# Two residual blocks with a mixture of experts on one core: the router with its weights stationary, the tokens' parts by quarters, the overflow count in eight parts, the gathers in other steps

## The reference

```python
def moe_swiglu(h, router, w1, w3, w2):        # h [256, 1024], 8 experts, top 2, d_ff 3584
    logits = (h @ router).astype(jnp.float32)
    top_v, top_i = lax.top_k(logits, TOP_K)
    gates = jax.nn.softmax(top_v, axis=-1).astype(h.dtype)
    ...
    def expert_block(args):
        xe, e = args
        return swiglu(xe, w1[e], w3[e], w2[e])    # (silu(x w1) * (x w3)) w2
    ...
    y = zeros.at[row_tok].add(yb * row_w[:, None])
```

## Time and profile before

| what | value |
|---|---|
| median of 3 runs | 2162.42 us (2159.96 to 2165.96) |
| profiled execution | 2167.47 us, its span 2166.1 us |
| granted TensorE clock, mean over the span | 0.976 |
| PE busy | 2086.6 us (96%) |
| DVE busy | 1711.0 us (79%) |
| ACT busy | 1260.6 us (58%) |
| chain that ended last | PE 84%, DVE 9%, ACT 4%, issue 3% |
| HBM traffic over the span | 267 GB/s |

### The profile page before, as it was taken

The page is one execution under the profiler, slowest core; times in us unless marked ns, Lnnn a source line. Parts: engine busy times, 40 slices in busy tenths (PEclk is TensorE's granted clock), DMA queues, the critical chain, the costliest instruction groups (busy, mean ns, idle before and its releaser), DMA issues.

```text
span 2166.1 us, 30863 instructions
## 1 busy us (share of the span) xinstructions
PE 2086.6 (96%) x12783; PEld 1859.6 (86%) x12783; DVE 1711.0 (79%) x1845; ACT 1260.6 (58%) x1270; POOL 39.8 (2%) x77
## 2 busy tenths in 40 slices
PE   5999999899999999999999999999999999999997
PEld 4887899899898999999998788887888878888886
DVE  6777696899767776777547888897898978898886
ACT  3457643545334454443446677776777767777775
POOL 3010000000000000000000000000000000000000
PEclk8999999899999999999999999999999999999999
DMA  9853576467763446888536999998999989999993
GB/s 307 274 164 111 171 240 205 148 213 251 235 204 136 155 151 210 296 280 276 186 125 243 324 349 365 359 360 317 354 364 357 359 314 353 360 366 366 359 372 148
DMA packets 332802, 580.73 MB, mean 268 GB/s; under 512 B 10357, under 2 KB 150155, under 8 KB 332656
## 3 DMA queue, kind: packets, MB, share of 16 engines
q1 hardware_dynamic: 329152, 572.57, 75.9%
q0 software_dynamic: 3008, 5.78, 1.2%
q10 hardware_dynamic: 496, 0.33, 0.1%
HBM read 577.56 MB, written 1.07 MB: 267 GB/s over the span
## 4 chain that ended last, share of the span: by engine, by line
PE 84%; DVE 9%; ACT 4%; issue 3%; DMA 0%; SPq 0%; DVEq 0%; ACTq 0%
PE bk L632 14%; PE bk L634 14%; PE bk L633 14%; PE bk L626 9%; PE bk L627 9%; PE bk L628 9%; DVE macc L1863 3%; DVE wlo L1836 2%; ACT whi L1256 2%; PE bk L703 1%; PE bk L1148 1%; PE bk L688 1%; PE bk L689 1%; PE bk L690 1%; DVE uc L2182 1%
## 5 line engine op out<-in xcount | busy, mean ns | idle before, releaser
L1836 DVE TENSOR_TENSOR wlo<-raw,whi 128x2048 fp32r<-128x2048 f32 x475 | 1081.0, 2277 | 281.2 <-ACT whi L1256 280.4
L1256 ACT CAST whi<-raw 128x2048 fp32r<-128x2048 f32 x475 | 902.6, 1901 | 405.4 <-PE bk L634 271.1
L626 PE MATMUL bk<-HH,whi 128*128 128x256 f32 x1480 | 430.4, 291 | 6.9 <-DVE HL L1909 6.2
L627 PE MATMUL bk<-HL,whi 128*128 128x256 f32 x1480 | 421.2, 285 | 0.0
L628 PE MATMUL bk<-HH,wlo 128*128 128x256 f32 x1480 | 420.8, 284 | 0.0
L632 PE MATMUL bk<-whi,xh 128*128 128x512 f32 x896 | 357.2, 399 | 4.9 <-DVE wlo L1836 4.9
L634 PE MATMUL bk<-wlo,xh 128*128 128x512 f32 x896 | 351.2, 392 | 0.0
L633 PE MATMUL bk<-whi,xl 128*128 128x512 f32 x896 | 350.7, 391 | 0.0
L626 PEld LDWEIGHTS bk<-HH,whi 128*128 128x128 f32 x1480 | 286.6, 194 | 11.4 <-issue 8.7
L627 PEld LDWEIGHTS bk<-HL,whi 128*128 128x128 f32 x1480 | 286.7, 194 | 1.6 <-issue 1.0
L628 PEld LDWEIGHTS bk<-HH,wlo 128*128 128x128 f32 x1480 | 286.4, 194 | 0.0
(11 more groups left out here) (366 smaller groups left out, 2606.4 us busy)
## 6 DMA issues: line engine op xcount, KB each, us to landing
raw<-in_moe_w SPq DMA_DIRECT2D x336, 1024.0 KB, 6.1
raw<-in_ada_w SPq DMA_DIRECT2D x48, 1024.0 KB, 5.3
raw<-in_ff_w SPq DMA_DIRECT2D x40, 1024.0 KB, 5.3
raw<-in_w_in SPq DMA_DIRECT2D x29, 1024.0 KB, 5.5
raw<-in_w_mod SPq DMA_DIRECT2D x24, 1024.0 KB, 5.6
raw<-in_w_up SPq DMA_DIRECT2D x22, 1024.0 KB, 5.1
raw<-in_attn_w_qkv SPq DMA_DIRECT2D x12, 1024.0 KB, 5.2
raw<-in_w_branch SPq DMA_DIRECT2D x8, 1024.0 KB, 5.3
```

The lines of the kernel that those rows point to most:

```text
L626: pe.matmul(o, sh, mh, start=start, stop=False, skip_group_check=True)
L627: pe.matmul(o, sh, ml, start=False, stop=False, skip_group_check=True)
L1256: act.copy(whi[k][:, :n], raw[q.slot[i]][:, :n]).then_inc(q.hi_done.mark(g), 1)
L1836: dve.tensor_tensor(wlo[k][:, :n], raw[q.slot[i]][:, :n], whi[k][:, :n].bitcast(F), ALU.subtract).then_inc(q.taken.mark(i), 1)
```

## The change

1. The logits: the router's chunk is stationary and all 256 tokens of H2 move, so the logits come out as 8 x 256. DVE copies them to SBUF (`LT`, in a part of `onat`), TensorE transposes them in two small transposes into a second bank ("lgt"), and DVE reads them there.
2. The tokens' transposes go by `quarters`: first the low four chunks of both halves, then the high four. The two small transposes stand behind the first quarter. DVE computes the first two quarters of TL ahead of the ranks, the other two behind PB. The first gather waits for two quarters at its chunk 0 and for the other two at its chunk 4, and has 4 spare matmuls ahead of it in place of 14.
3. The cast (ACT) and the split (DVE) of slab 138 + NP move to the end of the route, on ACT behind the exponential, on DVE behind the gates.
4. `dve_count` takes a part number and runs in steps 2 to 9, one part in each.
5. The gathers for the next pair are in steps i = 5, 6, 7 and 12, the gather's rest in step 13.

```diff
+        LT = onat[0:8, 0, 0:S]
...
+        quarters = ((0, 0), (1, 0), (0, 4), (1, 4))
+        gather_at = {5: 0, 6: 2, 7: 4, 12: 6}
...
@@ pe_route @@
-            for tb in range(2):
-                for k in range(8):
-                    pe.wait_ge(*(yield from act_step.of("h2", k)))
-                    t = pe.matmul(u.t[:, 8 * tb:8 * tb + 8], H2[:, k, tb * 128:tb * 128 + 128], rw[:, k, :], start=(k == 0), stop=(k == 7))
+            for k in range(8):
+                pe.wait_ge(*(yield from act_step.of("h2", k)))
+                t = pe.matmul(u.t[0:8, 0:S], rw[:, k, :], H2[:, k, :], start=(k == 0), stop=(k == 7))
             t.then_inc(u.fill(), 1)
-            for tb in range(2):
-                for c in range(0, 8, 4):
-...
+            for n, (tb, c) in enumerate(quarters):
+                u = take(X_G, "tok", tb, c)
+                for j in range(4):
+                    t = pe.transpose(u.t[:, j * 128:(j + 1) * 128], H2[:, c + j, tb * 128:tb * 128 + 128], ident)
+                t.then_inc(u.fill(), 1)
+                if n == 0:
+                    u = take(X_L, "lgt")
+                    pe.wait_ge(*(yield from N.of("lt")))
+                    for tb in range(2):
+                        t = pe.transpose(u.t[:, 8 * tb:8 * tb + 8], LT[0:8, tb * 128:tb * 128 + 128], ident[0:8, 0:8])
                     t.then_inc(u.fill(), 1)
...
@@ pe_gather @@
             if q is st and p == 0:
-                spare(us[0].t[:, 0:128], 14)
-                for n in range(4):
-                    pe.wait_ge(*(yield from N.of("tl", n)))
+                spare(us[0].t[:, 0:128], 4)
             pe.wait_ge(*(yield from dve_step.of("pb", q.name, p)))
             for c in chunks:
+                if q is st and p == 0 and c in (0, 4):
+                    for n in (c // 2, c // 2 + 1):
+                        pe.wait_ge(*(yield from N.of("tl", n)))
...
 @@ pe_experts (act_experts and dve_experts alike) @@
-                if p < 3 and 4 <= i < 8:
-                    yield from pe_gather(st, p + 1, M_T, (2 * i - 8, 2 * i - 7))
-                if p < 3 and i == 12:
+                if p < 3 and i in gather_at:
+                    yield from pe_gather(st, p + 1, M_T, (gather_at[i], gather_at[i] + 1))
+                if p < 3 and i == 13:
...
@@ act_route @@
-            yield from act_hi(st, 138 + NP)
-            for n in range(4):
-                tb, c = n // 2, n % 2 * 4
+            for n, (tb, c) in enumerate(quarters):
...
             act.activation(col(3), col(2), AF.Exp).then_inc(act_step.mark("gap"), 1)
+            yield from act_hi(st, 138 + NP)
...
@@ dve_route @@
-            yield from dve_lo(st, 138 + NP)
...
+            dve.tensor_copy(LT, u.t[0:8, 0:S]).then_inc(u.sem, 1)
+            N.note(("lt",), u.drained())
+            dve.wait_ge(*(yield from B.full("lgt")))
+            u = B.at["lgt",]
...
+            for n in range(2):
+                yield from tokens_low(n)
             dve.wait_ge(*(yield from B.full("rank")))
...
             yield from dve_pb(st, 0, lambda n, tb: RK[:, tb, n:n + 1])
-            for n in range(4):
-...
+            for n in range(2, 4):
+                yield from tokens_low(n)
...
             dve.tensor_tensor(gt, gt, tmp, ALU.add).then_inc(dve_step.mark("gates"), 1)
+            yield from dve_lo(st, 138 + NP)
...
 @@ dve_experts @@
-                if s_ == 2:
-                    yield from dve_count()
+                if 2 <= s_ < 10:
+                    yield from dve_count(s_ - 2)
```

More of the change, by code:

```diff
@@ L1079, in pe_route @@
             pe.wait_ge(*(yield from N.of("rw")))
-            for tb in range(2):
-                for k in range(8):
-                    pe.wait_ge(*(yield from act_step.of("h2", k)))
-                    t = pe.matmul(u.t[:, 8 * tb:8 * tb + 8], H2[:, k, tb * 128:tb * 128 + 128], rw[:, k, :], start=(k == 0), stop=(k == 7))
+            for k in range(8):
+                pe.wait_ge(*(yield from act_step.of("h2", k)))
+                t = pe.matmul(u.t[0:8, 0:S], rw[:, k, :], H2[:, k, :], start=(k == 0), stop=(k == 7))
             t.then_inc(u.fill(), 1)
-            for tb in range(2):
-                for c in range(0, 8, 4):
-                    u = take(X_G, "tok", tb, c)
-                    for j in range(4):
-                        t = pe.transpose(u.t[:, j * 128:(j + 1) * 128], H2[:, c + j, tb * 128:tb * 128 + 128], ident)
+            for n, (tb, c) in enumerate(quarters):
[8 more added lines that the diff above has]
+                        t = pe.transpose(u.t[:, 8 * tb:8 * tb + 8], LT[0:8, tb * 128:tb * 128 + 128], ident[0:8, 0:8])
                     t.then_inc(u.fill(), 1)
@@ L1771, in act_experts @@
                     yield from act_collect(st, s_ - 1, e - 1, (e - 1) // 2, (e - 1) % 2)
-                if p < 3 and 4 <= i < 8:
-                    yield from act_gather(st, p + 1, (2 * i - 8, 2 * i - 7), True)
-                if p < 3 and i == 12:
+                if p < 3 and i in gather_at:
+                    yield from act_gather(st, p + 1, (gather_at[i], gather_at[i] + 1), True)
+                if p < 3 and i == 13:
                     yield from act_ptt(st, p + 1)
@@ L2415, in dve_route, with tokens_low @@
             dve.tensor_tensor(col(2), col(1), col(0), ALU.subtract).then_inc(dve_step.mark("gap"), 1)
+            def tokens_low(n):
+                tb, c = quarters[n]
+                dve.wait_ge(*(yield from xhi_done.of("tok", n)))
+                u = B.at["tok", tb, c]
+                dve.tensor_tensor(TL[:, tb, c * 128:c * 128 + 512], u.t[:, :], TH[:, tb, c * 128:c * 128 + 512].bitcast(F),
+                                  ALU.subtract).then_inc(u.sem, 1)
+                N.note(("tl", n), u.drained())
+            for n in range(2):
+                yield from tokens_low(n)
             dve.wait_ge(*(yield from B.full("rank")))
@@ L2497, in dve_scatter, with dve_count @@
                     t.then_inc(dve_step.mark("x_moe"), 1)
-        def dve_count():
+        def dve_count(part):
             eix = misc[:, 256:264]
[L2502 to L2513, removed]
+            if part == 0:
+                dve.wait_ge(*(yield from B.full("count")))
+                u = B.at["count",]
+                dve.tensor_copy(CN[:, 0:8], u.t[:, 0:8]).then_inc(u.sem, 1)
+                dve.wait_ge(*u.drained())
+                dve.tensor_scalar(CN[:, 8:16], CN[:, 0:8], float(CAP), None, ALU.is_gt).then_inc(dve_step.mark("ov"), 1)
+                dve.memset(CN[:, 56:64], 1.0).then_inc(dve_step.mark("ov"), 1)
+                dve.wait_ge(*dve_step.now())
+                dve.tensor_tensor_scan(CN[:, 16:24], CN[:, 56:64], CN[:, 8:16], 0.0, ALU.mult, ALU.add).then_inc(dve_step.mark("ov"), 1)
+                dve.wait_ge(*dve_step.now())
+                dve.tensor_copy(CN[:, 48:49], CN[:, 23:24]).then_inc(dve_step.mark("ov"), 1)
+                dve.memset(OV[:, :, 3:4], -1.0).then_inc(dve_step.mark("ov"), 1)
+                return
+            if part == 7:
+                dve.wait_ge(*(yield from dve_step.of("ov")))
+                dve.tensor_copy(CI[:, :], CN[:, 48:52]).then_inc(dve_step.mark("ci"), 1)
+                return
+            j = (part - 1) // 2
+            sj, ej = CN[:, 24 + 8 * j:32 + 8 * j], CN[:, 49 + j:50 + j]
+            dve.wait_ge(*(yield from dve_step.of("ov")))
+            if part % 2:
                 dve.tensor_scalar(sj, CN[:, 16:24], float(j + 1), None, ALU.is_equal).then_inc(dve_step.mark("ov"), 1)
@@ L2522, in dve_count @@
                 dve.tensor_scalar(ej, ej, 7.0, None, ALU.min).then_inc(dve_step.mark("ov"), 1)
[L2523 to L2532, removed]
+                return
+            for tb in range(2):
+                dve.wait_ge(*dve_step.now())
+                dve.tensor_tensor_reduce(CN[:, 56:64], sj, RK[:, tb, :], 1.0, -float(CAP), ALU.mult, ALU.add,
+                                         OV[:, tb, j:j + 1]).then_inc(dve_step.mark("ov"), 1)
+                dve.wait_ge(*dve_step.now())
+                dve.tensor_tensor_reduce(CN[:, 56:64], sj, ro(tb, 7), 1.0, 0.0, ALU.mult, ALU.add,
+                                         OV[:, tb, 4 + j:5 + j]).then_inc(dve_step.mark("ov"), 1)
         def dve_experts():
```

## The result

The median went from 2163.89 us (four runs, 2159.96 to 2165.96) to 2139.95 (four runs, 2139.00 to 2141.42): ratio 0.9889, 95% interval 0.9872 to 0.9905. The forecast was 2141, range 2135 to 2150.

The account below looks back on a forecast made before the run. TensorE's matmuls set the experts' pace, so gains had to come from its waits. Gains of 6.7 + 11.8 + 4.6, less 0.5 for holds and 1.0 for the clock, gave 21.6 us: median 2162.4 to 2140.8, say 2141, range 2135 to 2150.

Parts of the forecast that it names:

- The count: Experts, step after the count, 23.69 us and 6.73 too much: spreading the count over steps 2 to 9 gains 6.7 us.
- 0.5 us allowed for new holds: Experts, steps 2 to 9: the inserted count parts hold TensorE up by 0.5 us in all; bounds 0 and 8.
- the slack read off at 1450.64: Experts, DVE: work inserted there put the next split 2.17 us later, yet its step took the undisturbed 17.46 us.
- The gathers: Experts, two two-step stretches with turns waiting for a bank: moving the gathers gains 5.55 + 6.29 = 11.8 us; bounds 7.4, 11.8.
- The route: Ahead of the experts, from logits to first expert: the shorter chain gains 4.6 us; bounds 6.8 and 1.6.
- 1.0 off for the clock: Experts' start: a low clock there costs 1.0 us; bounds 0 and 3.
- step (f): Route, gather: chunks 6 and 7 wait for banks emptied by DVE's XL copies, a hole of 2 us before chunk 6.
- a low stretch inside the gather: Route: hidden behind DVE, as six chunks would then take 5.7 us and end at 1142.6.
- Rival 1: Route: clock low from the rank to about 1148, experts start 3 us later, gain near 19, time 2144; chance 0.13.
- Rival 2: Experts: DMA can't hold 369 GB/s, most of the 18.5 us return as ACT's waits, time near 2158; chance 0.05.
- Rivals 3 and 4: Experts, steps 12 and 13: bank wait once per pair, 2159 us, chance 0.05; waits in both steps, 2176 us, chance 0.02.
- The sum: Whole kernel: 6.7 + 11.8 + 4.6 - 0.5 - 1.0 = 21.6 us gained.

Follow-up runs that it names:

- e5_count_halves: Kernel after, with the count's eight parts run four in step 2 and four in step 3; single execution 2145.16 us.
- e4_one_chunk: Kernel after, with the gathers' chunks 1, 2, 2, 2 and 1 in steps 4, 5, 6, 7 and 12; single execution 2139.45 us.
- e1_count: Kernel before, with only the count split into eight parts; median 2157.27 us, ratio to before 0.9973.
- e3_route: Kernel before, with only the new route (count and gathers as before); median 2155.01 us, ratio to before 0.9968.
- e11_after_again: Kernel after once more, unchanged, beside e9_spare_late; median 2141.84 us, ratio to before 0.9896.
- e2_gathers: Kernel before, with only the gathers moved to steps 5, 6, 7 and 12, their rest to 13; median 2152.29 us, ratio to before 0.9955.
- e6_old_logits: Kernel after, with the logits in their old form, without the copy and the two small transposes; single execution 2137.62 us.
- e8_spare: Kernel after, with three more spare matmuls ahead of the rank and seven in place of four ahead of the gather; single execution 2143.59 us.
- e9_spare_late: Kernel after, with the spare matmuls of e8_spare and DVE's third-slab split moved behind the XL copies; median 2140.45 us, ratio to before 0.9889.
- e7_slab_early: Kernel after, with the third slab's cast and split back in their old early place in the route; single execution 2145.98 us.

## Why the prediction was right

**The count** was to give 6.7 us: step 3 fell by 6.69. The 0.5 us allowed for new holds was not needed. DVE's heaviest piece (collection, part 5 and the turn's low part, in its program for step 7) runs from 1278.20 to 1280.98 in the profile after, which is behind the turn at 1274.80; the step from there to the next turn takes 17.47, against 17.46 before. So 2.8 us went unnoticed there, and the slack read off at 1450.64 in the earlier trace rows holds. e5_count_halves shows its end: 5.05 us of DVE work between two splits cost a wait of 2.5.

**The gathers** were to give 5.55 and 6.29. The two stretches of the earlier trace rows fell by 6.46 (41.87 to 35.41) and by 7.3, and steps 12 and 13 of the same pairs took on the 0.9 that was moved there: 5.5 and 6.3. That the bank was the cause is shown by e4_one_chunk. The size of the loss varies from execution to execution: what a pair of steps lost beyond its wait of 3.7 us was 5.55 - 3.7 = 1.9 and 6.29 - 3.7 = 2.6 us in the profile before, and by the steps' lengths in the same way (against 36.32) 1.9 and 0.2 in e1_count, 2.6 and 1.8 in e3_route. The bare waits, 7.4 us, are in all three; of the other 4.4, e1_count would have shown only 2.1. The varying part goes with the clock: from the end of the wait to the end of the pair it was granted at 1.00 on average where 0.2 us was lost, at 0.91 in the three cases with 1.8 or 1.9, and at 0.87 and 0.88 in the two with 2.6. So the prediction's assumption that every execution loses the full 11.8 does not hold; that it came out so near is in part luck.

**The route** was to give 4.6 with 1.0 off for the clock, 3.6; it gave 4.1. Up to the gather the sum holds to 0.1 us: lg copied at +4.50 (forecast 4.6), gather at +9.69 (9.8 to 9.9). Behind that two things came otherwise. In e11_after_again, with the clock at 1.00, the hole of step (f) is there with 1.6 us (2 forecast), but chunk 6 begins at +14.42 where the sum has 14.9, and the first expert comes at +16.72 where it has 17.2: several differences of about 0.1 us, all to the good. (The XL copies take 0.34 each when free to run, eight in 2.74, not 0.47; only the first of them stands in the sum, and chunk 6 began 0.47 after its start.) And in the profile after the low clock fell inside the gather and reached nearly to its end: chunk 6 began at 1138.97, with the XL copies already on their way, so the hole was not there, and the first expert came 0.8 us later than in e11_after_again. The prediction had called a low stretch inside the gather hidden behind DVE. By its own figures (six chunks at the low clock end at 1142.6, the bank is free at 1141.9) it would be hidden only in part. So the 1.0 us taken off for the clock had about the right size, 0.8, but it was lost in the gather and not, as reckoned, under the first experts.

**Rival 1** (the clock stays low from the rank into the first expert) came about in part: low through the gather, back at 1.00 before the first expert matmul. In after the clock was 1.00 in the stretch with the transposes (1128 to 1130) and fell only near 1133 (0.98 from 1132 to 1133, 0.50 from 1133 to 1134): behind the wait of 1.4 us, and ahead of the one of 0.6 us, which ended at 1133.68. By the rule of the Trainium skill ("TensorE: Matmul & The Clock Gate", Part 4) the transposes don't count as busy either; whether they had a part in the later fall, these runs do not separate from the wait. **Rival 2** (DMA) is out: a share of 1.01 at 372 GB/s, and ACT, which casts the slabs, has no wait for a load in all of the experts. **Rivals 3 and 4** (bank waits in steps 12 and 13) are out: 17.91 and 18.24, 17.92 and 18.23, 17.94 and 18.21 us in the three pairs.

**The sum** was 21.6, and the medians differ by 23.9, with an interval that holds both. The two profiles differ by 26.0 because 3.1 us lie ahead of the route. In the changed places they differ by 22.8 (18.7 and 4.1), 1.2 more than the sum: 0.5 from the holds that did not come, 0.5 from the route, 0.2 from the gathers.

## What to carry to other kernels

Take the cost of a step from its undisturbed fellows in the same trace, and price a wait as the whole excess of its step and the next; but count only the bare wait as certain, since the clock behind a wait of 3.7 us cost anything from 0.2 to 2.6 us here. When a ring of PSUM banks is shared, count the takes per step against its length: here scatter, gather and turn could share a step as long as no take needed a bank that was filled in that same step. Work that is spread over steps is free at least up to the largest insertion that went unnoticed in the trace (2.2 to 2.8 us here; 5.05 us cost a wait of 2.5).

## What the runs showed of the hardware

The granted clock differs from one execution to the next in the same place of the same code: 0.57 on average from 1132 to 1140 in the profile after, 1.00 in e11_after_again. So one profile can hide a wait (here 1.6 us for an XL copy) behind a slower TensorE. And the form of a small product decided over the clock for more than 12 us. In all four profiles with the old form (before, e1_count, e2_gathers, e6_old_logits) the granted clock was 1.00 until some 2 us after the first logits matmul, 0.50 from 4 us to 14 us after it, and 1.00 again from 16 us on, though TensorE waited for nothing in all that time. In all nine with the new form it was 1.00 for the first 8 us, though TensorE waited in them: 0.7 us in e8_spare and e9_spare_late, 1.4 us in six others, 3.0 us in e7_slab_early. The old form holds 128 x 128 blocks and moves 8 columns in a matmul, for 6.7 us; the new one holds 8 columns and moves 256, for 3.6 us. Which of these differences the clock goes by, these runs do not separate.
